# A bound on the row index of the routed gathers and scatters, and the scatter of a block ahead of a later block's gathers, in a mixture-of-experts layer

## The reference, cut to what matters

```python
_, idx = lax.top_k(scores + router_bias, TOP_K)          # 2048 tokens, TOP_K = 8
padded = (counts + ROW_BLOCK - 1) // ROW_BLOCK * ROW_BLOCK   # ROW_BLOCK = 128
row_tok = jnp.zeros((n_rows,), jnp.int32).at[dest].set(flat_tok[order])
row_w = jnp.zeros((n_rows,), jnp.float32).at[dest].set(flat_w[order])
xs = h[row_tok].reshape(n_blk, ROW_BLOCK, d)             # d = 1024, float32
ys = lax.map(expert_block, (xs, blk_e))                  # swiglu with hidden size 256
ys = ys * row_w[:, None]
return jax.ops.segment_sum(ys, row_tok, num_segments=t_tok)
```

## Time and profile before

| what | value |
|---|---|
| time before, median of 3 runs | 2853.92 us (2848.2 to 2861.36) |
| the profiled execution | 2842.91 us |
| its span in the trace | 2841.2 us |
| the loop over routed blocks in the trace | about 1263 to 2700 us |
| PE, share of the span | 94% |
| POOL, share of the span | 47% |

### The profile page before, as it was taken

How to read it: one execution, slowest core, us unless ns; L and a number is a source line. 1 busy time by engine, 2 the same in 40 slices (tenths; PEclk the granted TensorE clock), 3 DMA queues, 4 the chain that set the end, 5 groups by cost and what they waited for, 6 DMA issues and landing times.

```text
span 2841.2 us, 50420 instructions
## 1 busy us (share of the span) xinstructions
PE 2683.9 (94%) x11902; PEld 2177.7 (77%) x11903; DVE 1799.3 (63%) x2519; ACT 1218.4 (43%) x1738; POOL 1330.1 (47%) x1116
## 2 busy tenths in 40 slices
PE   7999999999999999559999999999999999999996
PEld 6888888788878887447777777877777788777875
DVE  5534555555555555557667766676776767667576
ACT  3233223223223232135555655555555555556432
POOL 3000002200230033557777777777777778777612
PEclk9999999999999999779999999999999999999998
DMA  8223333432343235159989989898998998898875
GB/s 305 93 96 115 130 104 98 132 134 98 101 137 137 97 104 170 60 172 267 265 248 268 286 244 256 235 261 246 275 265 246 269 257 255 244 253 251 219 232 188
DMA packets 169918, 554.82 MB, mean 195 GB/s; under 512 B 30145, under 2 KB 35889, under 8 KB 169873
## 3 DMA queue, kind: packets, MB, share of 16 engines
q1 hardware_dynamic: 95776, 344.42, 34.7%
q0 software_dynamic: 65888, 195.67, 29.1%
q10 hardware_dynamic: 8208, 14.16, 1.5%
HBM read 434.97 MB, written 119.18 MB: 195 GB/s over the span
## 4 chain that ended last, share of the span: by engine, by line
PE 34%; issue 7%; POOL 4%; DVE 3%; ACT 2%; DMA 2%; another core or an unknown queue 2%; ACTq 2%; DVEq 1%; POOLq 1%
PE ps_gu L1466 8%; PE ps_gu L1468 7%; PE ps_gu L1467 7%; PE ps_y L1468 3%; PE ps_y L1466 3%; PE ps_y L1467 3%; POOL xs L1412 3%; PE ps_h L1513 1%; ACT expert_hi L1543 1%; DMA acc_odd<-y,sidx 1%; DVE expert_lo L1648 1%; ACTq L1365 1%; DVEq L1673 1%; POOLq L94 0%
## 5 line engine op out<-in xcount | busy, mean ns | idle before, releaser
L1412 POOL DMA_INDIRECT xs<-h_dram,gidx x656 | 829.1, 1264 | 323.9 <-issue 191.7
L1466 PE MATMUL ps_gu<-expert_hi,xl 128*128 (+1 forms) x1392 | 570.8, 410 | 20.2 <-DVE xl L1664 18.9
L1467 PE MATMUL ps_gu<-expert_lo,xh 128*128 (+1 forms) x1392 | 555.3, 399 | 0.0
L1468 PE MATMUL ps_gu<-expert_hi,xh 128*128 (+1 forms) x1392 | 555.2, 399 | 0.0
L1648 DVE TENSOR_TENSOR expert_lo<-expert_raw,expert_hi 128x1024 f32 (+1 forms) x390 | 459.8, 1221 | 101.4 <-ACT expert_hi L1543 70.6
L917 DVE TENSOR_TENSOR ul<-raw,uh 128x1024 fp32r<-128x1024 f32 x186 | 227.9, 1225 | 402.9 <-ACT uh L741 380.4
L1543 ACT ACTIVATE expert_hi<-expert_raw 128x1024 f32 (+1 forms) x390 | 390.5, 1052 | 53.9 <-PEq L1517 42.8
L93 POOL TENSOR_SCALAR rstd<-mean 128x1 f32<-128x1 f32 x49 | 15.8, 323 | 843.5 <-ACT junk L760 828.6
L504 PE MATMUL ps_t<-hh,ul 128*128 128x512 f32 x1024 | 402.0, 393 | 3.1 <-DVE wgl L1146 3.1
L506 PE MATMUL ps_t<-hh,uh 128*128 128x512 f32 x1024 | 399.6, 390 | 0.0
L505 PE MATMUL ps_t<-hl,uh 128*128 128x512 f32 x1024 | 399.5, 390 | 0.0
(11 more groups left out here) (263 smaller groups left out, 3796.4 us busy)
## 6 DMA issues: line engine op xcount, KB each, us to landing
expert_raw<-experts SPq DMA_DIRECT2D x396, 512.0 KB
raw<-units SPq DMA_DIRECT2D x192, 512.0 KB
xs<-h_dram,gidx POOLq DMA_INDIRECT x656
h_dram<-h ACTq DMA_DIRECT2D x17, 512.0 KB
acc_odd<-h POOLq DMA_DIRECT2D x17, 512.0 KB, 14.8
acc<-x SPq DMA_DIRECT2D x4, 2048.0 KB, 8.1
expert_raw<-acc_odd SPq DMA_DIRECT2D x16, 512.0 KB, 6.6
expert_raw<-x POOLq DMA_DIRECT2D x14, 512.0 KB, 3.7
```

The source lines that it names most:

```text
L1412: nc.gpsimd.indirect_dma_start(xs[s][:, g * DQ:(g + 1) * DQ], None, h2_quarters, bass.IndirectOffsetOnAxis(ap=gidx[s][:, g:g + 1], axis=0) ...
L1466: nc.tensor.matmul(out_, sl, vh, start=first, stop=False)
L1467: nc.tensor.matmul(out_, sh, vl, start=False, stop=False)
L1468: return nc.tensor.matmul(out_, sh, vh, start=False, stop=last)
```

## The change

Two edits in the POOL part of `mixture`. First, the routed gathers and the scatters get a bound on the index: S * Q - 1 for the quarters of rows that the gathers read (Q = 4), S - 1 for the rows that the scatters add to. A row whose index is above the bound is left out by the DMA and is no error. The gathers of blocks 0 and 1 have no bound, so that both `xs` buffers are filled once; later a padded row keeps what an earlier block left in its place, and its output is not added anywhere. Second, in each iteration the scatter of block j-1 with its two waits now stands ahead of the gathers of block j+5 with theirs.

```diff
-            def gather(s):
+            def gather(s, **bound):
                 for g in range(Q):
                     nc.gpsimd.indirect_dma_start(
                         xs[s][:, g * DQ:(g + 1) * DQ], None, h2_quarters,
-                        bass.IndirectOffsetOnAxis(ap=gidx[s][:, g:g + 1], axis=0)).then_inc(xs_in[s], 16)
+                        bass.IndirectOffsetOnAxis(ap=gidx[s][:, g:g + 1], axis=0), **bound
+                        ).then_inc(xs_in[s], 16)
+
+            def gather_routed(s):
+                gather(s, bounds_check=S * Q - 1, oob_is_err=False)
 
             def scatter(s):
                 nc.gpsimd.indirect_dma_start(
                     accs[s], bass.IndirectOffsetOnAxis(ap=sidx[s][:, 0:1], axis=0), y[s][:, :], None,
-                    compute_op=ALU.add).then_inc(y_out[s], 16)
+                    bounds_check=S - 1, oob_is_err=False, compute_op=ALU.add).then_inc(y_out[s], 16)
...
                 if j >= 2:
                     pool.wait_ge(xs_turned, j - 1)
-                gather(j % 2)
+                    gather_routed(j % 2)
+                else:
+                    gather(j % 2)
             n = pairs(pool)
             with pool.Fori(0, n) as i:
                 for d in (1, 2):
                     s = d % 2
 
-                    pool.wait_ge(idx_ready, i * 2 + (d + 6))
-                    pool.wait_ge(xs_turned, i * 2 + (d + 4))
-                    carry(pool, marks)
-                    gather(1 - s)
-
-
                     pool.wait_ge(y_ready, i * 2 + (d + 2))
                     pool.wait_ge(y_out[1 - s], i * 16 + 16)
                     carry(pool, marks)
                     scatter(1 - s)
+
+                    pool.wait_ge(idx_ready, i * 2 + (d + 6))
+                    pool.wait_ge(xs_turned, i * 2 + (d + 4))
+                    carry(pool, marks)
+                    gather_routed(1 - s)
```

## The result

| | before | after |
|---|---|---|
| median of the runs | 2851.06 us (2838.91 to 2861.36, 4 runs) | 2771.17 us (2769.67 to 2775.35, 4 runs) |
| ratio, 95% interval | | 0.9726 [0.97, 0.9753] |
| profiled execution | 2842.91 us | 2770.64 us |
| its span | 2841.2 us | 2768.7 us |

The change makes the kernel 2.7% faster. The direction is as forecast. The size is not: 80 us between the medians, 72.5 us between the spans, where the prediction had 26.

The account below looks back on a forecast made before the run. The prediction took PE to bound the loop, with waits behind late scatters; 19.7 us of waits plus 6 us of slow clock gave 26 us off the 2853.9 us median, so 2828 us (chance 0.60), range 2797 to 2868 us.

Parts of the forecast that it names:

- What bounds the loop: Routed-block loop: PE is busy 1392.6 of 1437 us; order can give back at most 0.5 us a block, 79 us.
- The late landing: Scatters issued 9.3 us late land 8.3 us after issue, so ACT waits 61.1 us for `sidx`, 36 times.
- 19.7 + 6 = 26 us: Gain from the earlier scatter: 19.7 us of PE waits plus four stretches at the lower clock, 1.5 us each.
- the 13 waits: PE waits for `hid` that follow a late `sidx` with an expert opening in between, 19.7 us of 43.6.
- The scatter is not named there, and I count that part as untouched: 12 PE waits, 22.3 us, follow a late `hth` that the profile calls remote; no gain was counted for them.
- late `hth`: ACT's `hth` starts late although `ps_h` is long there, released by something called remote; ACT loses 68.3 us.
- The three waits that the prediction put to neither cause: PE waits among the 28 in the loop outside the 13 behind late `sidx` and 12 behind late `hth`.
- nine slow stretches: Loop stretches where PE runs at the lower clock behind a wait, each costing 1.5 us; four were counted as gain.
- more goes than the 13 waits: Rival: late `hth` hangs on POOL's order too, so all 43.6 us and nine slow stretches go; 2797 us, chance 0.08.
- The early scatter gives little: Rival: with `sidx` on time something else ends the same PE wait last; 8 us gained, 2846 us, chance 0.19.
- The bound: Index bound on POOL's gathers and scatters: no time taken either way; cover ends at 0.13 us for each DMA.
- Cover for the gathers: Gathers start up to 1.93 us later, 16.3 of 17.2 us used; nothing taken, 65 us at risk if cover goes.

Follow-up runs that it names:

- e3: Kernel before, old order and no bound, with the scatter adding only the first quarter of each row: 2784.98 us, ratio 0.9826.
- e11: Kernel before, with each weight piece from the third expert on bringing only a quarter of its columns: 2765.91 us, ratio 0.9898.
- e14: Kernel before, with each scatter held until `hth` of block j+1 is taken and adding only a quarter of each row: 2763.98 us, ratio 0.9866.
- e12: Kernel before, unchanged, profiled on a chip where it shows no late `hth`: median 2801.01 us, ratio 0.9999.
- e1: Changed kernel without any bound, so the new order alone: 2767.72 us, ratio 0.976 to the kernel before.
- e16: Kernel before, with each scatter held until `hth` of block j+1 is taken, on a chip with late `hth`: 2829.57 us, ratio 0.9875.
- e7: Changed kernel without the bound on the gathers, so new order with only the scatters bounded: 2771.14 us, ratio 0.968 to the kernel before.
- e8: Changed kernel run again without further edits: 2769.54 us, ratio 0.9681 to the kernel before.
- e2: Kernel before in its old order, with the bounds on routed gathers and scatters added: 2809.41 us, ratio 0.9924.
- e15: Kernel before, unchanged, profiled on a chip where it shows late `hth`: median 2860.14 us, ratio 0.9993.
- e17: Changed kernel run again without further edits, on a chip where the kernel before shows late `hth`: 2770.98 us, ratio 0.9681.
- e6: Kernel before, old order and no bounds, with each scatter adding only the first 32 of 128 rows: 2886.48 us, ratio 1.0092.
- e5: Kernel before, with SP held from looking up a block's expert until PE has done that block's `gate_up`: 2857.19 us, ratio 0.9976.
- sets 2 and 5: Two groups of follow-up runs, both on chip 1, each beside the kernel before, whose medians there were 2860.96 and 2862.71 us.

## Why the prediction was wrong, point by point

- **What bounds the loop**: right. A block without waits is 8.59 us before and after, and the most that an order could give, 0.5 us a block (79 us), is nearly what came (70).
- **The late landing**: right in mechanism. The scatter goes 0.9 us after `y` in the block shown, the 36 waits for `sidx` are gone, and e3, e11 and e14 show that an early landing alone takes them away (e3 all but 8.7 us). The 8.3 us of the prediction is a bad landing and not the usual one: e12's median is 7.0 us from the start of an issue of 1.6, so 5.4 behind its end.
- **Its size, "19.7 + 6 = 26 us"**: too small by a term that the sum does not have. A wait costs PE 0.5 us beyond itself (e12). The trace of the kernel before has it too: around the wait of 1.77 us at 1341.70 the blocks take 10.52 and 8.93 us, 0.5 us more than two steady ones and the wait. For the 13 waits that is some 7 us; for all 28 of the kernel before it is 14.
- **"The scatter is not named there, and I count that part as untouched"**: this is the step that failed. The 12 waits behind a late `hth`, 22.3 us in sum, hung on POOL's old order too. e1 shows it without the bound, e3 shows that the landing isn't what they hang on, and e16 that the scatter issued behind PE's hand-over is a good part of them. The three waits that the prediction put to neither cause, 1.6 us, belong to them too, one behind a `sidx` and two behind a late `hth`. So 14 waits and five of the nine slow stretches hung on the late `hth`: 23.7 + 14 x 0.5 + 5 x 1.5 = 38 us that were counted as nothing. With all waits gone the sum is 43.6 + 28 x 0.5 + 9 x 1.5 = 71 us, and the spans differ by 72.5.
- **The rival "more goes than the 13 waits"** had this mechanism, with 57 us and 0.08. The sign for it was in its own sentence: in most of the cases `hth` starts within 0.3 us of the end of a scatter's issue. I took a name that the profile can't place ("remote") as a reason to leave the rows out; the coincidence in time was the better evidence.
- **"The early scatter gives little"**: wrong; with `sidx` on time nothing else ends the wait last, as e14 beside e12 shows best.
- **The bound**: right. It is no gain and no loss in the new order (e1, e7, e8), its price is 0.02 to 0.07 us a gather (means and medians of e1 and e7 against e8), under the 0.13 us at which POOL would bind, and the queue is down to 164.39 MB. That it gives 0.8% in the old order (e2) was not foreseen.
- **Cover for the gathers**: taken at nothing, and right; in the changed kernel DVE waits for a gather 4 times in the whole span, 8.0 us, and never between 1263 and 2630 us.

**What stays open.** Why PE's signal reaches ACT late at all, why it does on some chips and not on others, and why only at some issues of POOL. I counted which issue is under way at PE's hand-over (taken 0.35 us after the transposes begin). In e15 it is the third gather in 64 blocks, 3 of them late, the last gather in 70, 28 of them late, and the scatter in 18, 14 of them late. In e16 all 29 late ones are among the 64 at the last gather. In the changed kernel the hand-over has moved: in e17 it meets the third gather 137 times (as the one at 1416.98 above), never late, and the last gather 16 times. By these counts part of the cure would be where the hand-over falls, which no run tests by itself. It can't be the whole, as e7, e8 and e17, on that chip, have 61 hand-overs at the last gather and 1 late among them; and on the chip of e12, 68 at the last gather and 36 at the scatter are all on time. e6, in which PE's signals were late more often with a smaller scatter, has no explanation. Excluded are SP's queue (e5), and the bytes and the landing of the scatter (e3).

## What to carry to other kernels

When a queue issues several transfers in a fixed order, put first the one whose source buffer someone is waiting to refill, and look in which stretch of the other engines' hand-overs each issue falls. Price a stall of PE at more than its own length: here 0.5 us came on top of every wait, and 1.5 us more where the clock fell. And an idle time whose releaser the profile can't name is to be counted by what happens at its end, and not left out of the sum; here the change that took away such waits also took away the difference between chips.

## What the runs showed of the hardware that was not expected

- The kernel before took 2795 us in one set and 2863 us in another, the kernels in the new order 2768 to 2771 us in each of four. Within a set the times agree, and sets 2 and 5, both on chip 1, have 2861 and 2863 us, so I put the difference down to the chip.
- A signal of PE can reach ACT 1.2 or some 2.7 us late while POOL issues indirect DMAs (45 of 156 blocks in e15), though PE's rows show its work on time (their ends are modelled, so PE itself may have been late).
- Rows above the bound keep their packets: 65888 in both kernels, with 7571 more that are under 512 bytes (37716 against 30145), near the 2 x 3840 rows left out; with the bound on the scatters alone (e7) they are 33984, 3839 more. A bounded gather has a move of 29 ns, hidden in the gap ahead of it, and takes 24 to 44 ns more of issue on average.
- A scatter of 32 of 128 rows (e6) made the kernel slower than one of 128, by 0.9%.
